# Retention of the second block: index scores, key choice and head finishing placed in pieces between the weight slabs

## Chip, cores and metric

The kernel runs on one core of one Trainium2 chip. The metric is the device time of one execution in microseconds (us).

## What is computed

Two transformer blocks for 512 tokens of width 1024 in fp32, one after the other. The second one works on 528 tokens (16 meta tokens in front): a SwiGLU, a mixer, a second SwiGLU and a norm. The change touches the mixer:

```python
proj = u @ w_in          # rq, rk, rv, rg, aq, ak, av, iq, ik, iw, g_ret, g_att
rq, rk = rope(rq), rope(rk) * RET_DK ** -0.5          # 4 heads of 256
yr = retention(rq, rk, rv)                            # decayed q k^T times v, 512 wide
yr = y * rsqrt(mean(y * y) + EPS)                     # at the end of retention, per head
yr = (silu(rg) * yr) @ w_ret_out
# index branch: which 128 keys a query may attend to
rel = relu(einsum('bqhd,bsd->bqhs', iq, ik))          # 8 heads of 64
score = einsum('bqh,bqhs->bqs', iw, rel) * idx_scale  # masked to earlier keys
_, sel = top_k(score, 128)
ya = attention(aq, ak, av, keys = meta + sel) @ w_att_out
merged = sigmoid(g_ret) * yr + sigmoid(g_att) * ya
out = merged @ w_mix_out
```

## The kernel before

**Slabs.** All projection weights come as slabs of 128 x 1024 fp32 (0.5 MB). SyncE's queue fetches them into six buffers (`raw_slabs`). ScalarE rounds each into one of four buffers (`slabs_rounded`, L1142, `split_ahead`), VectorE subtracts to get the remainder (`slabs_remainder`, L1744, `slab_remainder`), and TensorE multiplies: each product is the sum of three matmuls (rounded x rounded, rounded x remainder, remainder x rounded; L642, `Slab.add`). A slab of columns is 24 matmuls of 256 columns (272 in half 0), a slab of rows (values, `rows_of`) has matmuls of 512 columns: 12 in half 1, 18 in half 0. ScalarE may round slab q when TensorE has begun slab q - 3.

**The order.** Each engine runs its own program, written out by hand, in step with the others through semaphores. On ScalarE and VectorE a call of `point()` stands for one slab of TensorE's order: at slab t it prepares slab t + 3. What an engine has to do besides stands between the points, and holds back the points behind it.

**Two halves.** Block 2 runs twice: half 0 with 16 + 256 tokens (T = 272), half 1 with the other 256. During half 0 the first block's expert layer still goes on between the slabs (woven in by `woven_by`): GpSimd gathers a row of 2048 floats per token (L2484), VectorE takes a dot product (L1992) or, for every third row, also adds it up (L2041), ScalarE makes the coefficient and a diagonal matrix (L1295 to L1306), TensorE adds the row to its sums (L824, four matmuls of 512 columns). There, the projections have three PSUM banks (0 to 2); in half 1, where nothing is gathered, they have four (0 to 3), and the other products have banks 4 to 7.

**The mixer** (`mixer` of each engine). It begins with the index projections. Then come four retention heads of 12 slabs each: two query slabs, two key slabs, four value slabs, four gate slabs. Behind the query slabs VectorE ropes the queries (L2219 to L2229, `rope_pair`) and behind the key slabs the keys (in half 0, L2223 and L2224 read two banks); this frees the banks. After the key slabs of head 0 come the index scores: 16 matmul products with 64 rows (L957; 4 banks in half 0, 16 in half 1), relus of ScalarE out of PSUM (L1432), VectorE's weighted sum (L2181, L2187), the scale and the mask (L2195 to L2201). After the key slabs of head i > 0 TensorE sums the squares of head i - 1 (L967, `head_sums`) and VectorE finishes that head (`finish_head`): mean square (L2238), the root on ScalarE (L1419, `head_root`), reciprocal (L2243), two multiplies of 128 x 1024 (L2245, L2251). Then, in every head, VectorE makes four of the 16 rounds of key choice (`keep_keys`): MAX8 (L2208) finds the eight largest scores and MATCH_REPLACE8 (L2211) marks them. Only after that come the points of the four value slabs. After these TensorE computes the scores of the head (L996), VectorE multiplies in the decay (L2283, L2287), the gate slabs follow (L2300), then the value matmuls (L1008, L1011). After the four heads: four pairs of slabs for the retention gate (the last head is finished in the first pair, and the marks are turned into a mask, L2317 to L2320), 16 slabs of `w_ret_out` in four groups, merged with the gate (L2330), 8 value slabs, and the attention heads.

Of the kernel before, what the change touches and what calls it, by code (L numbers as in the profile page):

```python
# [16 lines left out]
P = 128  # L17
# [219 lines left out]
def index_heads(g):  # L237

    return (0, 2, 1, 3, 4, 6, 5, 7) if g == 2 else tuple(range(IDX_HEADS))

# [51 lines left out]
def build(nc, slabs_d, xT_d, memT_d, metaT_d, vecs_d, consts_d, consts16_d, subk_d, wi_d, peer_uv_d, out_d,  # L292
          n_slabs):
    ctx = ExitStack()
    with ctx:
# [313 lines left out]
        def _(pe):  # L609
# [276 lines left out]
            def two(x, off, n, since=None, per=1):  # L886

                b = claim(gm)
                for d in range(2):
                    one(x, off, n, b, d * n, None if d else since, per, d == 1)  # L890

            def rows_of(x, off, meta):
# [3 lines left out]
                for s in range(KT // 2):  # L896
                    w = slab()
# [31 lines left out]
            def mixer(h, r):  # L929
# [14 lines left out]
                def index_scores():  # L944
# [4 lines left out]
                    for j, tt in enumerate(h.judged):  # L949
                        w = (h.first + tt + 1) * P  # L950
                        g = 2 if 2 * w <= 512 else 1
                        for head in range(0, IDX_HEADS, g):
# [7 lines left out]
                            m.then_inc(bank_full[b], 1)  # L960

# [7 lines left out]

                for i in range(RET_HEADS):  # L970
                    two(x, h.off, HALF)
                    if h.off:
                        one(x, 0, h.T, claim(gm))
                        one(x, 0, h.T, claim(gm))
                    else:
                        two(x, 0, HALF)
                    if i == 0:
                        index_scores()
                    else:
                        head_sums(i - 1)  # L980
                    v_banks = rows_of(x, h.off, h.off)
# [133 lines left out]
        def _(act):  # L1115
# [297 lines left out]
            def mixer(h, r):  # L1413
# [7 lines left out]
                def index_relus():  # L1421
# [3 lines left out]
                    for j, tt in enumerate(h.judged):  # L1425
                        w = (h.first + tt + 1) * P
                        g = 2 if 2 * w <= 512 else 1
                        for head in range(0, IDX_HEADS, g):
# [5 lines left out]
                            n += 1  # L1434

# [7 lines left out]
                at.take()  # L1443
                for i in range(RET_HEADS):
                    n = RET_HEADS * h.n + i
                    gm.take()
                    for _ in range(2 if h.off else 1):
                        gm.take()
                    points(4)
                    if i == 0:  # L1450
                        index_relus()
                        act.wait_ge(index_scored, h.n + 1)
                        if h.n == 0:
                            keep(K_IK, r.ik, kept_index)
                    else:
                        head_root(i - 1)
                    banks = [gm.take(), gm.take()]
                    meta = at.take() if h.off else None
                    points(4)
# [188 lines left out]
        def _(dve):  # L1648
# [476 lines left out]
            def mixer(h, r):  # L2125
# [42 lines left out]
                def index_scores():  # L2168
# [24 lines left out]
                    dve.wait_ge(relu_read, n)  # L2193
# [39 lines left out]
                def finish_head(i):  # L2233
# [7 lines left out]
                    dve.sem_inc(ret_ms, 1)  # L2241
                    dve.wait_ge(ret_root, n + 1)
# [4 lines left out]
                                                  op0=ALU.mult, op1=ALU.mult))  # L2247
                    sync()
# [3 lines left out]

                for i in range(RET_HEADS):
# [7 lines left out]
                    points(2)  # L2261
# [3 lines left out]
                    if i == 0:  # L2265
                        index_scores()
                    else:
                        finish_head(i - 1)
                    for _ in range(KEEP // 8 // RET_HEADS):
                        keep_keys()  # L2270
# [3 lines left out]
                    points(4)  # L2274
# [19 lines left out]
                    for e in range(2):  # L2294
                        bn = gm.take()
                        points(2)
# [14 lines left out]
                for c in range(4):  # L2311
                    last_gate = gm.take()
                    points(2)
                    if c == 0:
                        finish_head(RET_HEADS - 1)
                        for j, w, tt in judged:
                            step(dve.tensor_scalar(work(tt, w), work(tt, w), TAKEN, HIDE, ALU.not_equal, ALU.mult))  # L2317
                        if h.n == 0:
                            step(dve.tensor_scalar(work(0, P), tri[:, :], -HIDE, HIDE, ALU.mult, ALU.add))
                        step(dve.memset(r.key_bias[:, :, 0:META], 0.0))  # L2320
                        sync()
                    elif c < 3:
                        rests(4 * c - 4, 4 * c)
                for c in range(4):
# [3 lines left out]
                    if c == 0:  # L2328
# [3 lines left out]
                                             op0=ALU.add, op1=ALU.mult).then_inc(bank_free[b], 1)  # L2332
                for _ in range(2):
# [311 lines left out]
```

## Time and profile before

| | us |
|---|---|
| median of 3 runs | 3811.61 (3810.2 to 3816.32) |
| profiled execution | 3811.19 |
| its span, first to last instruction | 3809.4 |
| TensorE busy | 3330.7 (87%) |
| VectorE busy | 2566.6 (67%) |
| ScalarE busy | 1521.3 (40%) |
| GpSimd busy | 872.7 (23%) |
| retention heads of half 0 | about 1898 to 2176 |
| retention heads of half 1 | about 3081 to 3337 |

The profile is of one execution. Its page gives busy times and the costliest groups of instructions. The trace behind it is asked for waits (which engine waited for what), for the chain of waits (from the last instruction back to what released each one), for timelines of one engine and for busy times by stretch. All times are counted from the start of the span. A wait for several semaphores is put down to the one that came last.

### The profile page before, as it was taken

What the parts mean: (1) busy time and instruction counts of PE and PEld (TensorE: products, weight loads), DVE (VectorE), ACT (ScalarE), POOL (GpSimd) and SP (SyncE); (2) the same over time, 40 slices, a digit from 0 to 9 for tenths busy, and PEclk for the clock granted to TensorE, in tenths of its full rate; (3) what the DMA queues carried; (4) which work ended last, traced back from release to release, by engine and by line L of the source; (5) the groups of instructions that cost most, each with busy time, mean ns of one, the idle gap of its engine ahead of it and who ended that gap; (6) DMA issues with size and microseconds to landing.
All of it is one profiled execution on the core that took longest, in us unless ns stands there. A gap on an engine that the chain in (4) does not pass through costs nothing.

```text
span 3809.4 us, 48792 instructions
## 1 busy us (share of the span) xinstructions
PE 3330.7 (87%) x17936; PEld 2570.4 (67%) x17936; DVE 2566.6 (67%) x4483; ACT 1521.3 (40%) x3015; POOL 872.7 (23%) x596
## 2 busy tenths in 40 slices
PE   6998979896777777699999999888979988899898
PEld 4886767682222222488777776667869977799898
DVE  5997241386676767687777677778765575558665
ACT  3222333323333333444444444544444433344443
POOL 1001333335656565222222232122100000000000
PEclk9999989998999999899999999999989999899999
DMA  3222222227999999699888898788746633253354
GB/s 110 94 94 72 83 83 85 72 83 324 420 382 418 385 421 397 261 381 388 344 315 322 306 388 341 284 320 343 301 148 224 193 115 115 97 177 120 124 187 155
DMA packets 178834, 901.87 MB, mean 237 GB/s; under 512 B 20944, under 2 KB 26320, under 8 KB 112672
## 3 DMA queue, kind: packets, MB, share of 16 engines
q0 software_dynamic: 73728, 536.90, 35.3%
q1 hardware_dynamic: 94640, 341.88, 26.0%
q10 hardware_dynamic: 10240, 20.12, 1.6%
q8 instruction: 136, 2.23, 0.2%
q14 instruction: 90, 0.74, 0.1%
HBM read 891.02 MB, written 7.80 MB: 236 GB/s over the span
## 4 chain that ended last, share of the span: by engine, by line
PE 63%; DVE 15%; DMA 7%; issue 7%; POOL 6%; ACT 3%; ACTq 0%; DVEq 0%; POOLq 0%
PE psum L642 49%; PE psum L824 8%; DMA buffer_float<-in_peer_uv,buffer_uint 6%; POOL buffer_float L2484 6%; DVE buffer_bfloat L1992 2%; PE psum L1011 1%; DVE buffer_float32r L1668 1%; DVE buffer_float L1705 1%; DVE slabs_remainder L1744 1%; DVE norm_mean_square L1698 1%; ACT slabs_rounded L1142 1%; PE psum L996 1%; DVE buffer_float L1941 1%; DVE norm_recip_root L1676 1%; PE psum L1093 1%
## 5 line engine op out<-in xcount | busy, mean ns | idle before, releaser
L642 PE MATMUL psum<-buffer_float32r,slabs_rounded 128*128 128x256 f32 (+2 forms) x9376 | 2026.4, 314 | 88.4 <-DVE buffer_float32r L1668 67.4
L642 PEld LDWEIGHTS psum<-buffer_float32r,slabs_rounded 128*128 128x128 f32 x9376 | 1534.3, 191 | 256.9 <-issue 149.6
L642 PE MATMUL psum<-buffer_float32r,slabs_remainder 128*128 128x256 f32 (+2 forms) x4688 | 1437.6, 307 | 0.0
L1744 DVE TENSOR_TENSOR slabs_remainder<-raw_slabs,slabs_rounded 128x1024 fp32r<-128x1024 f32 x570 | 695.7, 1224 | 498.5 <-ACT slabs_rounded L1142 491.9
L824 PE MATMUL psum<-buffer_float,buffer_float 128*128 128x512 f32 x1712 | 848.9, 624 | 186.1 <-ACT buffer_float L1306 159.3
L1142 ACT ACTIVATE slabs_rounded<-raw_slabs 128x1024 fp32r<-128x1024 f32 x650 | 683.5, 1056 | 738.0 <-PE psum L642 639.5
L2484 POOL DMA_INDIRECT buffer_float<-in_peer_uv,buffer_uint x512 | 679.2, 1327 | 1178.0 <-PE psum L824 650.3
L642 PEld LDWEIGHTS psum<-buffer_float32r,slabs_remainder 128*128 128x128 f32 x4688 | 895.4, 191 | 40.4
L1992 DVE CUSTOM_DVE_ANT_0 buffer_bfloat<-buffer_float,buffer_float 128x1024 bf16<-128x1024 f32 x512 | 625.8, 1222 | 236.9 <-DMA buffer_float<-in_peer_uv,buffer_uint 231.6
L824 PEld LDWEIGHTS psum<-buffer_float,buffer_float 128*128 128x128 f32 x1712 | 306.5, 196 | 614.7 <-issue 606.6
L2471 POOL TENSOR_TENSOR slabs_remainder<-raw_slabs,slabs_rounded 128x1024 fp32r<-128x1024 f32 x80 | 193.3, 2428 | 667.1 <-ACT slabs_rounded L1142 666.9
L1295 ACT ACTIVATE buffer_float<-buffer_float 128x1 f32<-128x1 f32 x512 | 100.9, 197 | 483.9 <-DVE buffer_float L1992 483.2
L642 PE MATMUL psum<-slabs_rounded,buffer_float32r 128*128 128x512 f32 (+1 forms) x608 | 192.7, 404 | 52.9 <-DVE slabs_remainder L1744 37.7
L1306 ACT ACTIVATE buffer_float<-fixed,buffer_float 128x128 f32<-128x128 f32 x428 | 172.0, 402 | 40.6 <-ACT buffer_float L1299 1.9
L642 PEld LDWEIGHTS psum<-slabs_rounded,buffer_float32r 128*128 128x128 f32 x608 | 116.4, 201 | 85.4 <-DVE slabs_remainder L1744 39.5
L1129 ACT ACTIVATE buffer_float32r<-buffer_float 128x256 fp32r<-128x256 f32 (+3 forms) x232 | 110.9, 495 | 137.7 <-DVE buffer_float L1705 55.7
L1782 DVE SCALAR_TENSOR_TENSOR buffer_float<-buffer_float,vecs,buffer_float 128x512 f32<-128x512 f32 x232 | 158.4, 748 | 0.0
L1299 ACT ACTIVATE buffer_float<-buffer_float,buffer_float 128x1 f32<-128x1 f32 x512 | 150.9, 295 | 16.9
L1668 DVE TENSOR_TENSOR buffer_float32r<-buffer_float,buffer_float32r 128x256 fp32r<-128x256 f32 (+2 forms) x232 | 118.7, 525 | 19.8 <-ACT buffer_float32r L1129 17.5
L642 PE MATMUL psum<-slabs_remainder,buffer_float32r 128*128 128x512 f32 (+1 forms) x304 | 117.6, 387 | 0.0
L2041 DVE SCALAR_TENSOR_TENSOR buffer_float<-buffer_float,buffer_float,buffer_float 128x1024 f32<-128x1024 f32 x82 | 105.1, 1282 | 0.0
L698 PE MATMUL psum<-norm_recip_root,fixed 128*128 128x256 f32 (+2 forms) x32 | 18.6, 673 | 96.2 <-DVE norm_recip_root L1676 86.4
(201 smaller groups left out, 1922.4 us busy)
## 6 DMA issues: line engine op xcount, KB each, us to landing
raw_slabs<-in_slabs SPq DMA_DIRECT2D x650, 512.0 KB, 3.7
buffer_float<-in_peer_uv,buffer_uint POOLq DMA_INDIRECT x512, 9.7
buffer_float<-kept ACTq DMA_DIRECT2D x1, 5248.0 KB, 17.9
xT<-in_xT ACTq DMA_DIRECT2D x4, 512.0 KB, 10.8
buffer_float<-in_consts ACTq DMA_DIRECT2D x8, 256.0 KB, 3.8
kept<-buffer_float ACTq DMA_DIRECT2D x4, 512.0 KB, 4.3
kept<-buffer_float ACTq DMA_DIRECT2D x4, 272.0 KB, 3.1
kept<-buffer_float ACTq DMA_DIRECT2D x8, 136.0 KB, 3.8
```

The costliest lines, as they stand in the source:

```text
L642: m = pe.matmul(out, a, b, start=start and j == 0, stop=stop and j == 2)
L824: m = pe.matmul(psum[:, b, :], diag[:, slot, :], uv_rows[slot][:, D + q * 512:D + (q + 1) * 512], start=p == 0, stop=p == PICKS - 1)
L1129: act.activation(dst, src, ACT.Copy).then_inc(rounded, 1)
L1142: act.activation(slab_h[:, j, :], raw[:, r, :], ACT.Copy).then_inc(slab_rounded, 1)
L1299: act.activation(coefs[:, slot:slot + 1], acts[:, slot:slot + 1], ACT.Copy, scale=gates[:, tt, p:p + 1])\
L1306: act.activation(diag[:, slot, :], ident[:, :], ACT.Copy, scale=coefs[:, slot:slot + 1])\
L1668: dve.tensor_tensor(dst, src, high.bitcast(F32), ALU.subtract).then_inc(split, 1)
L1744: dve.tensor_tensor(slab_l[:, r, :], raw[:, r, :], slab_h[:, j, :].bitcast(F32), ALU.subtract)\
L1782: step(dve.scalar_tensor_tensor(out=acc, in0=cfp[:, h, t:t + S], scalar=w, in1=acc, op0=ALU.mult, op1=ALU.add))
L1992: dve.tensor_tensor_reduce(dump, uv_rows[slot][:, 0:D], hrow[tt], 1.0, 0.0, ALU.mult, ALU.add, dots[:, slot:slot + 1]).then_inc(dotted, 1)
L2471: pool.tensor_tensor(slab_l[:, r, :], raw[:, r, :], slab_h[:, j, :].bitcast(F32), ALU.subtract)\
L2484: pool.indirect_dma_start(uv_rows[slot], None, peer_uv_d, bass.IndirectOffsetOnAxis(eidx[:, tt, p:p + 1], 0))\
```

## The change

It does these things, in both halves:

- TensorE (`index_scores` becomes a generator): the banks of index scores are computed some at a time, two before each of the two key slabs of head 0, and in half 1 also three before each of its four value slabs (`index_banks`). ScalarE's relus and VectorE's weighted sums stand in the same places, before the point of that slab. Scale and mask (`index_done`) come after the value slabs' points.
- ScalarE writes the index keys to memory after those points, and waits for their rope alone instead of for the finished scores.
- VectorE finishes head i - 1 in three pieces: the mean square after the key rope, as before; reciprocal and first multiply after the point of value slab 0; second multiply after that of value slab 1.
- The 16 rounds of key choice: none in head 0; in each of heads 1 to 3 one after the points of value slabs 2 and 3 and one between the two points of each gate pair; the last four after the four merged groups of `w_ret_out`.
- The marks are turned into the mask after these.

The diff (empty lines and some unchanged ones left out):

```diff
@@ -237,6 +237,11 @@
+def index_banks(h):
+    return (2, 3) if h.n else (2, 0)
@@ -883,17 +888,21 @@
-            def two(x, off, n, since=None, per=1):
+            def two(x, off, n, since=None, per=1, before=None):
...
                 for d in range(2):
+                    if before:
+                        before()
                     one(x, off, n, b, d * n, None if d else since, per, d == 1)
-            def rows_of(x, off, meta):
+            def rows_of(x, off, meta, before=None):
...
                 for s in range(KT // 2):
+                    if before:
+                        before()
                     w = slab()
@@ -958,6 +967,7 @@
                             m.then_inc(bank_full[b], 1)
+                            yield
@@ -967,18 +977,32 @@
+                scoring = index_scores()
+                def scores_in_k():
+                    for _ in range(index_banks(h)[0]):
+                        next(scoring)
+                def scores_in_v():
+                    for _ in range(index_banks(h)[1]):
+                        next(scoring)
...
                     if h.off:
-                        one(x, 0, h.T, claim(gm))
-                        one(x, 0, h.T, claim(gm))
+                        for _ in range(2):
+                            if i == 0:
+                                scores_in_k()
+                            one(x, 0, h.T, claim(gm))
                     else:
-                        two(x, 0, HALF)
+                        two(x, 0, HALF, before=None if i else scores_in_k)
+                    if i:
+                        head_sums(i - 1)
+                    v_banks = rows_of(x, h.off, h.off, None if i else scores_in_v)
                     if i == 0:
-                        index_scores()
-                    else:
-                        head_sums(i - 1)
-                    v_banks = rows_of(x, h.off, h.off)
+                        assert next(scoring, None) is None
                     own = [(r.rk, h.off + tt * P, r.rv[:, tt], tt * P) for tt in range(2)]
@@ -1432,6 +1456,7 @@
                             n += 1
+                            yield
@@ -1441,22 +1466,30 @@
                 at.take()
+                scoring = index_relus()
                 for i in range(RET_HEADS):
...
                     gm.take()
+                    points(2)
                     for _ in range(2 if h.off else 1):
                         gm.take()
-                    points(4)
-                    if i == 0:
-                        index_relus()
-                        act.wait_ge(index_scored, h.n + 1)
-                        if h.n == 0:
-                            keep(K_IK, r.ik, kept_index)
-                    else:
+                    for _ in range(2):
+                        for _ in range(0 if i else index_banks(h)[0]):
+                            next(scoring)
+                        point()
+                    if i:
                         head_root(i - 1)
...
                     meta = at.take() if h.off else None
-                    points(4)
+                    for _ in range(4):
+                        for _ in range(0 if i else index_banks(h)[1]):
+                            next(scoring)
+                        point()
+                    if i == 0:
+                        assert next(scoring, None) is None
+                        if h.n == 0:
+                            act.wait_ge(idx_rope, 3)
+                            keep(K_IK, r.ik, kept_index)
                     if h.off and i:
@@ -2190,7 +2223,12 @@
                             n += 1
-                    dve.wait_ge(relu_read, n)
+                            yield
+                def index_done():
+                    n = sum(IDX_HEADS // (2 if 2 * w <= 512 else 1) for _, w, _ in judged)
+                    dve.wait_ge(relu_read, 4 * h.n + n)
                     for j, w, tt in judged:
@@ -2239,17 +2277,20 @@
                     dve.sem_inc(ret_ms, 1)
+                    yield
                     dve.wait_ge(ret_root, n + 1)
...
                                                   op0=ALU.mult, op1=ALU.mult))
+                    yield
                     sync()
...
+                scoring = index_scores()
                 for i in range(RET_HEADS):
@@ -2258,20 +2299,30 @@
                     ks = [gm.take() for _ in range(2 if h.off else 1)]
-                    points(2)
+                    for _ in range(2):
+                        for _ in range(0 if i else index_banks(h)[0]):
+                            next(scoring)
+                        point()
                     if h.off and i:
...
                     rope_pair(r.rk, [full(bn) for bn in ks], h.T, 0)
-                    if i == 0:
-                        index_scores()
-                    else:
-                        finish_head(i - 1)
-                    for _ in range(KEEP // 8 // RET_HEADS):
-                        keep_keys()
+                    if i:
+                        finishing = finish_head(i - 1)
+                        next(finishing)
                     gm.take(), gm.take()
...
                         at.take()
-                    points(4)
+                    for p in range(4):
+                        for _ in range(0 if i else index_banks(h)[1]):
+                            next(scoring)
+                        point()
+                        if i and p < 2:
+                            next(finishing, None)
+                        elif i:
+                            keep_keys()
+                    if i == 0:
+                        assert next(scoring, None) is None
+                        index_done()
                     dve.wait_ge(decay_loaded, 32 * (n + 1))
@@ -2293,7 +2344,10 @@
                         bn = gm.take()
-                        points(2)
+                        point()
+                        if i:
+                            keep_keys()
+                        point()
                         b = full(bn)
@@ -2312,13 +2366,8 @@
                     if c == 0:
-                        finish_head(RET_HEADS - 1)
-                        for j, w, tt in judged:
-                            step(dve.tensor_scalar(work(tt, w), work(tt, w), TAKEN, HIDE, ALU.not_equal, ALU.mult))
-                        if h.n == 0:
-                            step(dve.tensor_scalar(work(0, P), tri[:, :], -HIDE, HIDE, ALU.mult, ALU.add))
-                        step(dve.memset(r.key_bias[:, :, 0:META], 0.0))
-                        sync()
+                        for _ in finish_head(RET_HEADS - 1):
+                            pass
                     elif c < 3:
@@ -2330,6 +2379,13 @@
                                              op0=ALU.add, op1=ALU.mult).then_inc(bank_free[b], 1)
+                    keep_keys()
+                for j, w, tt in judged:
+                    step(dve.tensor_scalar(work(tt, w), work(tt, w), TAKEN, HIDE, ALU.not_equal, ALU.mult))
+                if h.n == 0:
+                    step(dve.tensor_scalar(work(0, P), tri[:, :], -HIDE, HIDE, ALU.mult, ALU.add))
+                step(dve.memset(r.key_bias[:, :, 0:META], 0.0))
+                sync()
                 for _ in range(2):
```

## Rows read from the trace of the kernel before

**Rows 1.** The page: busy time by engine; two groups: busy us, mean ns | idle before.
```profile
PE 3330.7 (87%) x17936; PEld 2570.4 (67%) x17936; DVE 2566.6 (67%) x4483; ACT 1521.3 (40%) x3015; POOL 872.7 (23%) x596
...
L1744 DVE TENSOR_TENSOR slabs_remainder<-raw_slabs,slabs_rounded 128x1024 fp32r<-128x1024 f32 x570 | 695.7, 1224 | 498.5 <-ACT slabs_rounded L1142 491.9
...
L1142 ACT ACTIVATE slabs_rounded<-raw_slabs 128x1024 fp32r<-128x1024 f32 x650 | 683.5, 1056 | 738.0 <-PE psum L642 639.5
```

**Rows 2.** Waits of TensorE, 3070 to 3400 us: total, times, longest.
```profile
PE psum L642 <- DVE slabs_remainder L1744: 37.7, 4, 9.6
```

**Rows 3.** Chain of waits, 3150 to 3215 us: start us, us, what.
```profile
3153.02 11.37 PE psum L642 x96
3164.41 0.69 DVE buffer_float L2219
...
3167.72 1.76 DVE norm_mean_square L2243
...
3170.77 1.23 DVE buffer_float L2251
...
3182.82 1.24 DVE slabs_remainder L1744
...
3184.10 5.35 PE psum L642 x12
3189.45 4.20 PE psum L996 x20
3193.65 11.35 PE psum L642 x96
```

**Rows 4.** Busy time of three stretches: width, engines, granted clock, DMA share, GB/s.
```profile
3160.00:3190.00 30.00, 20.40 (x97) 16.41 (x96) 24.20 (x41) 8.01 (x9) 0.00 (x0) 0.83 0.31 104
3190.00:3220.00 30.00, 30.00 (x204) 26.92 (x203) 10.61 (x13) 10.87 (x14) 0.00 (x0) 1.00 0.35 114
...
1910.00:1925.00 15.00, 13.35 (x67) 10.02 (x66) 13.75 (x28) 4.65 (x10) 3.11 (x4) 0.89 0.93 373
```

**Rows 5.** Waits of TensorE, 1880 to 2260 us.
```profile
PE psum L824 <- ACT buffer_float L1306: 4.8, 2, 3.5
PE psum L824 <- issue: 4.5, 2, 2.9
PE psum L642 <- issue: 4.3, 2, 2.6
```

**Rows 6.** Timeline of TensorE in half 0: start, us, instruction [idle before].
```profile
1914.26 2.94 PE L957 MATMUL psum<-buffer_float,buffer_float 64*128 64x256 f32 x16
1918.85 3.21 PE L824 MATMUL psum<-buffer_float,buffer_float 128*128 128x512 f32 x4 [1.65 <-issue]
...
1990.42 0.71 PE L642 MATMUL psum<-slabs_rounded,buffer_float32r 128*128 128x512 f32 x2 [2.57 <-issue]
```

**Rows 7.** Timeline of VectorE in half 0.
```profile
1918.25 0.43 DVE L2224 TENSOR_TENSOR buffer_float<-psum,buffer_float 128x272 f32<-128x272 f32 x1
...
1919.87 0.35 DVE L2181 TENSOR_SCALAR buffer_float<-buffer_float,buffer_float 128x256 f32<-128x256 f32 x1
1920.25 3.83 DVE L2187 SCALAR_TENSOR_TENSOR buffer_float<-buffer_float,buffer_float,buffer_float 128x256 f32<-128x256 f32 x7
...
1925.35 0.43 DVE L2208 MAX8 buffer_float<-buffer_float 128x8 f32<-128x256 f32 x1
...
1926.55 0.43 DVE L2208 MAX8 buffer_float<-buffer_float 128x8 f32<-128x256 f32 x1
...
1989.84 0.43 DVE L2224 TENSOR_TENSOR buffer_float<-psum,buffer_float 128x272 f32<-128x272 f32 x1
```

**Rows 8.** L957 alone, in its two stretches of half 1: width, PE and PEld busy.
```profile
3093.07:3095.86 2.79, 2.78 (x12) 1.28 (x12) 1.00 0.04 15
3097.53:3105.31 7.78, 7.77 (x20) 2.95 (x20) 1.00 0.00 0
```

**Rows 9.** Waits of VectorE, 1880 to 2260 us.
```profile
DVE buffer_bfloat L1992 <- DMA buffer_float<-in_peer_uv,buffer_uint: 20.5, 13, 3.8
```

## The prediction

> **What bounds the kernel now.** I read the page first [rows 1]: TensorE is busy for 87% of a span of 3809.4 us and is the engine on which the chain mostly runs, so an edit pays only where TensorE stands still or runs at the lower clock. The edit touches the retention of block 2, which runs once per half of the tokens. So I took TensorE's waits in the two stretches, the chain of waits in the second, and then single instructions of VectorE.
>
> Half 1 (3060 to 3410 us): TensorE waits 37.7 us in four waits of up to 9.6 us, and all four are for a slab remainder of VectorE [rows 2]. One of them in the chain [rows 3]: VectorE ropes the keys from 3164.41, finishes the head before (mean square, reciprocal at 3167.72, two wide multiplies), does four rounds of key choice from 3172.00 on, 2.7 us each, and only then, at 3182.82, makes the remainder that the fourth value slab waits for; TensorE resumes at 3184.10. VectorE is not short of time: in 3190 to 3220 us it is busy 10.6 us of 30 [rows 4]. It does 18 us of other work in one piece, while only three slabs of 2.8 us are prepared ahead. The wait costs more than itself: in the stretch with the wait the mean granted clock is 0.83 against 1.00 in the next [rows 4], so part of it is at the lower of the two levels (1.2 instead of 2.4 GHz), and the fourth value slab takes 5.35 us [rows 3].
>
> Half 0 (1880 to 2260 us) is another case: expert rows are gathered and added between the slabs there. TensorE waits 13.6 us in six waits, none for a remainder [rows 5]. At head 0 it stops at 1917.20, after the index matmuls (1914.26 + 2.94), and goes on at 1918.85; at head 1 it goes on at 1990.42 after 2.57 us [rows 6]. In both cases VectorE's four reads of the key banks have just ended: at 1918.68 and at 1990.27 [rows 7]. Half 0 has only three banks for projections, and the second value bank is a key bank: the value slabs can't start before the keys are roped. The finishing and the key choice come behind that rope, and while VectorE does them (1919 to 1930 us) TensorE has its prepared slabs and these of 4.2 us or more (18 matmuls in half 0, and gathered rows between). They cost nothing there today.
>
> **Half 1, heads 1 to 3.** The change removes no instruction; it puts a slab remainder between the pieces. I walk one head from the start of its first query slab, with four slabs in 11.35 us, so 2.8 us a slab, and score matmuls of 4.20 us [rows 3]. Head sums and three value slabs fill 10.1 us (from 11.37 us after 3153.02 to 9.6 us before 3184.10), so the head sums take 1.7 us. TensorE without waits: value slabs at 13.1, 15.9, 18.7 and 21.3, scores at 24.1, gate slabs at 28.3, 31.1, 34.0 and 36.8. VectorE: key rope and mean square as now, and the root is back at 14.7 (3167.72). Behind the root ScalarE rounds the fourth value slab (1.06 us, [rows 1]) and VectorE's remainder (1.22 us, [rows 1]) is ready at 17.0; needed at 21.3. Reciprocal and first multiply (3.05 us) to 20.1, next remainder (gate slab 0) 21.3, second multiply (1.23 us) 22.5, remainder 23.7, one choice 26.4, remainder 27.6, one choice 30.3, five decay multiplies of at most 256 columns (0.43 us each, the row of L2224 [rows 7]) 32.5, the remainder of the last gate slab 33.7; needed at 36.8. That is the tightest place, 3.1 us to spare; the others have 4 to 7. The two choices between gate slabs end at about 43, and the next head begins at 49, after the value matmuls, so they are covered. ScalarE's gate tanh waits for the finished head (22.5) and needs its bank only at 34: covered. So both parts of the cost go: 9.6 us of wait and 5.35 - 2.8 = 2.55 us of slow slab, 12.15 us a head, **36.4 us** for three.
>
> **Half 1, head 0.** Now 12 index matmuls take 2.78 us, and after a wait of 1.7 us 20 more take 7.77 us [rows 8]: 12.2 us. Then come three value slabs, a wait of 8.9 us (37.7 less three of 9.6) and the slow slab (2.5 us). After the change two banks stand before each key slab and three before each value slab. Cost on TensorE alone: not under 2.78 / 6 = 0.46 us a bank, 7.4 us for 16; not over today's 12.2 us. The 20 paced by VectorE give 0.78 us a bank for the wider ones; I take 8 x 0.46 + 8 x 0.72 = 9.5 us, nearer to the lower end because slabs now cover ScalarE's copies. VectorE has three banks of 0.78 us and a remainder of 1.22 us in each value step, 3.6 us, against 3 x 0.6 + 2.8 = 4.6 us on TensorE. Gain 8.9 + 2.5 + 2.7 = **14.1 us** (11.4 to 16.2). The choice rounds of head 0 move behind the last gate: four, each after one merged pair. There TensorE has four slabs of 2.8 us per pair and VectorE 4 x 1.22 us, a multiply of this size out of PSUM (0.69 us, as at 3164.41 [rows 3]) and 2.7 us, 8.3 in all: hidden, with three slabs ready when the choice starts. If that cover failed, each could cost up to 2.7 us, 11 us.
>
> The TensorEngine Tiling page of the Trainium skill (Key Properties) says that a change of tiling mode drains TensorE; the change enters and leaves the 64-row form six times per half 1 instead of once, and twice in half 0. The trace of before shows one entry and one exit a half, both inside the 12.2 us and the 2.94 us above. By the page twelve more drains would make the time longer, by what a drain costs, which no row isolates; the upper bound of 12.2 us holds it, and the sum stays.
>
> **Half 0, head 0.** Here the change adds. The index matmuls (2.94 us, [rows 6]) move ahead of the key slabs, and VectorE's scoring (from 1919.87 to 1924.08, 4.2 us [rows 7]) moves ahead of the key rope, on which the value slabs wait. VectorE is busy nearly without a break there: 13.75 of 15 us from 1910 to 1925 [rows 4]. So the banks are read out some 4.1 us later (1922.8 instead of 1918.7), and the matmuls that used to fill that time are done before: TensorE idles about 5.8 us in place of 1.65. Behind it VectorE is 6 us ahead of today, which buys nothing, since nothing was late. Bounds: 0, if VectorE catches up before the key slabs end, and 4.2 + 2.94 = 7.1 us, if scoring and index matmuls add in series; a gain has no place, since nothing that ends the wait comes earlier. Taken, near the row that VectorE is full: +4.1 us, and +0.4 us for a longer stay at the lower clock (the 1.65 us wait already made four matmuls take 3.21 us [rows 6]).
>
> **Half 0, the rest.** Heads 1 to 3 keep the same wait for the rope; the pieces behind it are only interleaved: 0. The four choices that go behind the gates are 1.2 us each (1925.35 to 1926.55 [rows 7]), between a gathered row and its dot, in a stretch where VectorE waits for gathers (20.5 us in 13 waits [rows 9]). Between 0 and 4.8 us; I take +0.5. The mask multiplies move from the first gate to behind the last: 0, with 0.5 us of VectorE at stake.
>
> **Sum.** -36.4 - 14.1 + 4.5 + 0.5 = -45.5 us. The profiled execution took 3811.2 us (3809.4 us of span); the median of the runs shown is 3811.6, 0.4 us above. 3811.6 - 45.5 = 3766 us, 1.2% faster.
>
> **The rivals.**
> A. Part of the stall comes back. For: 3.1 us to spare before the last gate slab, and ScalarE's rounding now stands behind relus and the root. If a wait of 2.5 us with 2.5 us of slow clock stays in each of four heads, 20 us are lost: 3786 us.
> B. The gathers of half 0 lose more. For: dots wait for landings in 13 places. If each of the ten choices moved next to gate slabs or merges (six and four) holds up a row by its 1.2 us, 12 us in place of 0.5: 3777 us.
> C. Half 0 gains as well: its waits (13.6 us) close and head 0 costs nothing, because the gathers bound it and absorb the delay: 3811.6 - 50.5 - 13.6 = 3748 us. Against: the waits end with the rope.
> D. The wait of half 1 isn't VectorE's order but moves with it: at the end of its pieces VectorE is again more than three slabs (8.5 us) late, before the last gate slab, in each head. Then 9.6 + 2.5 us stay per head, and half 0 pays 5 us and B's 11.5: 3828 us, slower. It decides from 3.1 us more VectorE work before that slab for any wait at all, and from some 13 us for the whole of it; the walk leaves no place for 13 us.
> E. The change doesn't do what it says (the wait is put down wrongly to the remainder and stays): 3811.6 + 5 = 3817 us, within 0.2%. Against: all four have the same pattern.
>
> **How the numbers follow.** Forecast 0.62, A 0.13, B 0.10, C 0.08, D 0.03, E 0.04. Range: downwards the forecast with its bounds (head 0 at -16.2, half 0 at 0) is 3759, and some way to C; upwards through B to A: 3755 to 3788. Two tenths are left for C's end, the outer part of A, D and E. What a measurement of this kernel can tell from no change is about 0.2% or 7.6 us: faster 0.93, same 0.04, slower 0.03.
>
> **What would show it.** Right: in half 1 TensorE's waits for remainders fall from 37.7 us to under 3, heads follow each other in 49.2 us instead of 61.3, the value slabs run at 1.00 granted clock, choice rounds stand singly between remainders. In half 0 the wait before the value slabs of head 0 grows from 1.65 to about 5.8 us, the others stay at 1.7 to 2.9. Wrong: a wait for a remainder before the last gate slab (A, D), longer waits for landings after 2220 us (B), or no longer wait at head 0 of half 0 (C).

## The result

| | before | after |
|---|---|---|
| median, us | 3813.28 (3810.2 to 3816.32, 4 runs) | 3767.48 (3763.24 to 3771.78, 4 runs) |
| ratio | | 0.9879, 95% interval 0.9866 to 0.9892 |
| span of the profiled execution | 3809.4 | 3761.4 |

The change makes the kernel 1.2% faster, 45.8 us by the medians and 48.0 us by the two spans. The forecast was 3766 us, 45.5 us less. By the interval the gain lies between 41 and 51 us.

In half 1 the stall is gone. Where [rows 2] had 37.7 us of waits for a remainder, the waits of TensorE in the profile of the change from 3070 to 3360 us are an empty list. The chain of waits of the change from 3144 to 3195 us (start us, us, what) now stays on TensorE through the whole of head 1, where [rows 3] went over VectorE for 20 us:

```profile
3144.16 11.36 PE psum L647 x96
3155.52 1.73 PE psum L977 x8
3157.24 11.20 PE psum L647 x48
3168.44 4.20 PE psum L1020 x20
3172.64 11.36 PE psum L647 x96
...
3193.35 1.65 PE psum L647 x14
```

(L647 are the slabs, L977 the head sums, L1020 the scores; L642, L967 and L996 of before.) Four value slabs take 11.20 us without a break. From head to head it is 49.19 us (3144.16 to 3193.35) instead of the 61.3 us of before. The busy time by stretch of the change, in the head of the chain above and behind it (width, PE, PEld, DVE, ACT, POOL, granted clock, DMA share, GB/s) shows VectorE busy in both stretches, for 25.7 and 20.1 us, and the clock at 1.00 in both. In [rows 4] the stretch with the wait has 0.83 and the next one 1.00:

```profile
3160.00:3190.00 30.00, 30.00 (x179) 25.34 (x178) 25.74 (x42) 12.08 (x14) 0.00 (x0) 1.00 0.38 124
3190.00:3220.00 30.00, 30.00 (x179) 25.81 (x178) 20.10 (x26) 12.25 (x14) 0.00 (x0) 1.00 0.45 150
```

The timeline of VectorE in the change, in that head (start, us, instruction), shows how: a remainder (L1777) stands between the pieces, which are reciprocal (L2282) with the first multiply (L2284), the second multiply (L2291), and each choice (L2246, L2249).

```profile
3160.96 1.75 DVE L2282 RECIPROCAL norm_mean_square<-norm_recip_root 128x256 f32<-128x256 f32 x1
3162.74 1.23 DVE L2284 SCALAR_TENSOR_TENSOR buffer_float<-buffer_float,norm_mean_square 128x1024 f32<-128x1024 f32 x1
3163.88 1.22 DVE L1777 TENSOR_TENSOR slabs_remainder<-raw_slabs,slabs_rounded 128x1024 fp32r<-128x1024 f32 x1
3165.02 1.22 DVE L2291 TENSOR_TENSOR buffer_float<-buffer_float,buffer_float 128x1024 f32<-128x1024 f32 x1
3166.15 1.22 DVE L1777 TENSOR_TENSOR slabs_remainder<-raw_slabs,slabs_rounded 128x1024 fp32r<-128x1024 f32 x1
3167.29 1.15 DVE L2246 MAX8 buffer_float<-buffer_float 128x8 f32<-128x384 f32 x2
...
3175.73 1.21 DVE L1777 TENSOR_TENSOR slabs_remainder<-raw_slabs,slabs_rounded 128x1024 fp32r<-128x1024 f32 x1
```

In half 0 the wait before the value slabs of head 0 has grown. First the chain of waits of the change, on TensorE; before, [rows 6] had a wait of 1.65 us there:

```profile
1911.83 1.07 PE psum L966 x8
1912.90 3.20 PE psum L647 x24
1916.10 6.41 issue
1922.52 3.75 PE psum L829 x4
```

VectorE's timeline in the change, in the same stretch; before, [rows 7] had the rope's last read at 1918.25:

```profile
1911.19 0.35 DVE L2214 TENSOR_SCALAR buffer_float<-buffer_float,buffer_float 128x256 f32<-128x256 f32 x1
...
1916.57 2.11 DVE L2220 SCALAR_TENSOR_TENSOR buffer_float<-buffer_float,buffer_float,buffer_float 128x256 f32<-128x256 f32 x4
...
1921.92 0.43 DVE L2262 TENSOR_TENSOR buffer_float<-psum,buffer_float 128x272 f32<-128x272 f32 x1
```

The scoring (L2214, L2220) stands ahead of the key rope, whose last read of a bank (L2262) is 3.7 us later than before and ends at 1922.35. TensorE idles 6.41 us and goes on at 1922.52. Its next four matmuls take 3.75 us; the granted clock from 1922.5 to 1926.3 is 0.50, the lower level.

To see where time goes and comes back, one can compare when the same matmul of the slabs starts in each trace. Each column is the difference to before, in us; the runs of the last columns are described below.

```
place (start in before)              change  half1_only  half0_only  scores_late_half0  rope_first
half 0, head 0, 1st value slab done  +4.8    +0.5        +5.5        -0.5               -3.9      (1932.4)
half 0, first gate pairs             +3.6    +4.0        +7.5        -1.2               -10.2     (2202.4)
end of half 0's mixer and after      +0.4    -0.2        +2.9        -3.2               -11.7     (2593.0)
half 1, head 0, key slabs            +4.4    +2.5        +5.3        -0.9               -10.8     (3083.0)
half 1, retention gate               -45.4   -47.6       +6.2        -51.1              -61.2     (3320.5)
last matmul                          -48.0   -50.3       +6.4        -53.8              -64.0     (3795.7)
```

(The label's last number is the place's start in the trace of before.) The stretch between the first and the third row is not the same twice even for one piece of code (all differences are to the one profile of before): half1_only has the order of before in half 0, and is 4.0 us behind at one place and 0.2 us ahead at the next. Six profiles with the change's code in half 0 have +0.4, +2.8, +2.9, +6.0, +6.8 and +6.8 us in the third row. From its key slabs on, half 1 repeats: the eight profiles with the change's order there gain 49.7 to 50.5 us between the fourth row and the fifth. Heads 1 to 3 alone (3132.1 to 3320.5 of before) gain 36.57 us in each of these eight and in scores_late_half1.

### The profile page after: what moved, and what is told of

It is laid out like the page before. It is cut to its first block, busy times and chain, and to the rows that moved or that the text cites. A ratio compares the mean times of both kernels' runs of the same rounds, so it can differ in the third digit from the quotient of the medians.

```text
span 3761.4 us, 48792 instructions
## 1 busy us (share of the span) xinstructions
PE 3318.8 (88%) x17936; PEld 2560.1 (68%) x17936; DVE 2562.1 (68%) x4483; ACT 1519.6 (40%) x3015; POOL 866.5 (23%) x596
## 4 chain that ended last, share of the span: by engine, by line
PE 66%; DVE 12%; DMA 7%; issue 6%; POOL 6%; ACT 3%; ACTq 0%; DVEq 0%; POOLq 0%
PE psum L647 51%; PE psum L829 8%; DMA buffer_float<-in_peer_uv,buffer_uint 6%; POOL buffer_float L2540 6%; DVE buffer_bfloat L2025 2%; DMA raw_slabs<-in_slabs 1%; PE psum L1035 1%; DVE norm_mean_square L1731 1%; ACT slabs_rounded L1166 1%; DVE buffer_float L1738 1%; DVE buffer_float32r L1701 1%; PE psum L1020 1%; DVE buffer_float L1974 1%; DVE norm_recip_root L1709 1%; PE psum L1117 1%
## 5 line engine op out<-in xcount | busy, mean ns | idle before, releaser
L647 PE MATMUL psum<-buffer_float32r,slabs_rounded 128*128 128x256 f32 (+2 forms) x9376 | 2027.6, 314 | 89.5 <-DVE buffer_float32r L1701 67.6
L647 PEld LDWEIGHTS psum<-buffer_float32r,slabs_rounded 128*128 128x128 f32 x9376 | 1533.4, 191 | 260.6 <-issue 152.2
L647 PE MATMUL psum<-buffer_float32r,slabs_remainder 128*128 128x256 f32 (+2 forms) x4688 | 1436.1, 306 | 0.0
L1777 DVE TENSOR_TENSOR slabs_remainder<-raw_slabs,slabs_rounded 128x1024 fp32r<-128x1024 f32 x570 | 696.5, 1224 | 505.9 <-ACT slabs_rounded L1166 497.5
L647 PEld LDWEIGHTS psum<-buffer_float32r,slabs_remainder 128*128 128x128 f32 x4688 | 895.0, 191 | 40.7
L647 PE MATMUL psum<-slabs_rounded,buffer_float32r 128*128 128x512 f32 (+1 forms) x608 | 184.8, 390 | 14.3 <-POOL slabs_remainder L2527 10.9
L647 PEld LDWEIGHTS psum<-slabs_rounded,buffer_float32r 128*128 128x128 f32 x608 | 111.6, 193 | 46.0 <-issue 15.2
L1701 DVE TENSOR_TENSOR buffer_float32r<-buffer_float,buffer_float32r 128x256 fp32r<-128x256 f32 (+2 forms) x232 | 118.7, 526 | 20.1 <-ACT buffer_float32r L1153 17.8
L647 PE MATMUL psum<-slabs_remainder,buffer_float32r 128*128 128x512 f32 (+1 forms) x304 | 113.9, 375 | 0.0
## 6 DMA issues: line engine op xcount, KB each, us to landing
xT<-in_xT ACTq DMA_DIRECT2D x4, 512.0 KB, 10.6
```

Source lines behind the costliest of these rows:

```text
L647: m = pe.matmul(out, a, b, start=start and j == 0, stop=stop and j == 2)
L1701: dve.tensor_tensor(dst, src, high.bitcast(F32), ALU.subtract).then_inc(split, 1)
L1777: dve.tensor_tensor(slab_l[:, r, :], raw[:, r, :], slab_h[:, j, :].bitcast(F32), ALU.subtract)\
```

## The experiments

Each run was measured beside executions of the kernel before. Their medians are 3812.3, 3812.8 and 3813.0 us in the three groups of runs, and 3813.3 us beside the change. The change itself was not measured again, so a comparison with it is across groups. One kernel measured twice in this way (rope_first, rope_first_again) gave 3753.8 and 3749.2 us. So a difference under about 5 us between two runs needs the traces beside it.

**One half at a time.** The variants share one file in which the number of score banks before the key slabs, behind them and before the value slabs is a triple, and finishing and choices can be whole or in pieces, for each half.

half1_only:
```diff
-    return (2, 3) if h.n else (2, 0)
+    return (2, 0, 3) if h.n else (0, 4, 0)     # key slabs, behind them, value slabs
+PIECES = (False, True)
```

> The change in half 1 alone, half 0 in the order of before. Theory 1 (a ledger by stretch: half 1 gives 49 us, half 0 costs 4 to 5 us up to 2200 us, and the stretch behind it, bound by gathers, gives all but 0.5 us back): 48 to 49 us less than before, about 1 us less than the full change. Theory 2 (the pieces of half 0 earn what its early scores cost): the same as the full change, 46 to 48 us less than before. Rival to both (half 0's delay is paid for in full): 5 us less than the full change, 51 us less than before.

Measured: 3763.07 us, ratio 0.987 (0.9853 to 0.9886), 49.2 us less than before. That is nearest to theory 1, but the interval (44 to 56 us less) leaves the rival in and theory 2 too.

half0_only:
```diff
+    return (0, 16, 0) if h.n else (2, 0, 0)
+PIECES = (True, False)
```

> The change in half 0 alone, half 1 in the order of before. Theory 1: TensorE 4 to 5 us later than before at 2200 us, 0 to 1 us later from 2320 us on; the whole within 1 us of before. Theory 2: later by 4 us only up to the second head, nothing left at 2200 us. If the delay is paid for in full: 5 us longer than before at the end. In half 1 all four waits for remainders are there, 37.7 us.

Measured: 3816.56 us, ratio 1.0009 (0.9999 to 1.0018), 4.3 us more than before, in 10 runs against 14; the interval just takes in no change. Half 0's cost is there in the trace (first row, +5.5), and TensorE ends 6.4 us late. The waits of TensorE in half0_only from 3060 to 3420 us (engine, line, waited for: us, times, longest us) have the four of before again:

```profile
PE psum L650 <- DVE slabs_remainder L1785: 37.7, 4, 9.6
```

So the gain is half 1's. Theory 1 had it from the one profile of the change that half 0's cost is given back behind it: that profile has the smallest third row of the six. In the mean of the six the cost at the end of half 0 is 4.3 us, and it is 4.3 us by these medians. This speaks against theory 1, though neither settles it: the six spread over 6.4 us and stand against one profile of before. The next run gives more.

**Scores late in half 0.**
```diff
+    return (2, 0, 3) if h.n else (0, 4, 0)
```

> The full change, but in half 0 all four banks of index scores stay behind the key slabs and VectorE's scoring behind the key rope. Theory 1: the wait before the value slabs of head 0 is 1.7 us again instead of 6.4, TensorE is 4 us ahead of the full change until 2200 us, and behind the gather-bound stretch less than 1 us ahead: 47 us less than before. Theory 2: the 4 us stay: 51 us less than before.

Measured: 3757.79 us, ratio 0.9855 (0.9839 to 0.9872), 54.5 us less than before (49 to 61), and its last matmul is 5.9 us ahead of the change's. The wait before the value slabs of head 0, 6.41 us in the change, is back to that of before, by the waits of TensorE in this run from 1900 to 1935 us:

```profile
PE psum L829 <- issue: 1.7, 1, 1.7
```

Theory 1's 47 us lie outside the interval and theory 2's 51 us inside it: the cost of the early scores isn't given back. With half0_only and rope_first_early (below) three comparisons by medians say so, by 4.3 to 8.7 us, each run taken against its own before; each of them alone is weak. That the pieces of half 0 earn something of their own is a hint only: with scores late they put this run 3 us ahead of half1_only in the third row and 3.5 us in the last, which is within the spread of that stretch.

**Pieces off in half 1.** PIECES = (True, False), score banks as in the change.

> The full change, but in half 1 heads 1 to 3 finish the head before and make four choices in one piece behind the key rope, as before (scores stay between the slabs, the four choices of head 0 stay behind the gates). If the wait was this one piece: 9.6 us of wait and 2.5 us of slow slab come back in each of three heads, 36.4 us more than the full change, 11 us less than before. If the scores had been part of it in these heads too, less than 36 us comes back.

Measured: 3799.87 us, ratio 0.9965 (0.995 to 0.9979), 12.4 us less than before. Three waits are back, by the waits of TensorE in this run from 3060 to 3420 us:

```profile
PE psum L650 <- DVE slabs_remainder L1780: 29.1, 3, 9.9
```

The chain of waits of the same run shows one, with 5.49 us for the slab behind it:

```profile
3180.46 1.24 DVE slabs_remainder L1780
...
3181.74 5.49 PE psum L650 x12
```

Its profile is of the slowest of its five executions (3810.8 us) and is 10.6 us behind before at the key slabs already, so the stretch is counted from behind these. From 3105.2 to 3320.5 of before it gains 4.2 us where the change gains 41.9: 37.7 us for three heads, against 36.4 in my sum. The one piece of VectorE work was the wait.

**Scores late in half 1.** `return (0, 16, 0) if h.n else (2, 0, 0)`, pieces on in both halves.

> The full change, but in half 1 all 16 banks of index scores stay between the key slabs and the value slabs of head 0, as before; finishing and choices in pieces, no choice in head 0. My theory: TensorE spends 12.2 us on them again where it spends 9.1 us now in the full change, and VectorE's scoring ends before the fourth value slab is due (no choice behind it), so the wait of 8.9 us shrinks to under 1 us: 3 to 5 us more than the full change. Rival: the placing of the scores had removed the wait of head 0, and most of 8.9 + 2.5 us comes back: 12 to 14 us more.

Measured: 3769.81 us, ratio 0.9889 (0.9866 to 0.9911). No wait for a remainder is back, only the one for a relu between the index matmuls (waits of TensorE in this run, 3060 to 3420 us):

```profile
PE psum L966 <- ACT buffer_float L1459: 1.7, 1, 1.7
```

From 3083.0 to 3132.1 of before it gains 11.4 us, the change 13.3. So putting the scores between the slabs is worth 1.9 us in the traces, where 3 to 5 us were expected (2.8 us by the medians); the rest of head 0's gain comes with the choices leaving it. The rival's 12 to 14 us are out.

**How much slack.** Idle MAX8 instructions on VectorE, ahead of the decay multiplies in heads 1 to 3 of half 1:

```diff
+                    if h.n and i:
+                        for _ in range(4):        # 11 in slack_9us
+                            step(dve.max(r.top8[:, 1, :], work(1, 4 * P)))
+                            sync()
```

> The full change, with four idle MAX8 of 128x512 on VectorE (0.8 us each with their wait, 3.2 us) before the decay multiplies of heads 1 to 3 in half 1; their result is not used. In the trace of the full change the remainder of the last gate slab is ready at 3176.94 and the slab begins at 3180.9, 4.0 us of slack (my walk had 3.1). If the walk's reading is right, 3.2 us more cost nothing: no wait for a remainder in half 1, head after head 49.2 us. If VectorE's total load were the limit, each head would be 3 us longer.

Measured: 3770.53 us (one run), no wait for a remainder in half 1, and its heads start at 3123.98, 3173.16 and 3222.35: 49.18 us each, as in the change. The 2.9 us (4 x 0.73) disappear in the slack.

> The same with eleven idle MAX8, 8.9 us. Only what is over 4.0 us shows: a wait for the remainder of the last gate slab of 4.9 us in each of heads 1 to 3, and up to 2.5 us of low clock behind it, 15 to 22 us in all. If the slack were a matter of the head's total, no wait would come, since VectorE is idle for over 8 us later in the same head.

Measured: 3778.84 us (one run), and three waits, in the list of TensorE's waits from 3060 to 3420 us:

```profile
PE psum L647 <- DVE slabs_remainder L1777: 11.7, 3, 4.1
```

The chain of waits of this run shows the first of them, in front of the last gate slab:

```profile
3179.80 0.70 DVE buffer_float L2328
...
3182.39 1.14 DVE slabs_remainder L1777
...
3183.57 5.49 PE psum L647 x24
```

Each idle MAX8 turned out to take 0.73 us, so 8.0 us were put in. In the change the remainder for this slab is ready at 3176.94 (3175.73 + 1.21, above) and the slab starts at 3172.64 + 3 x 2.84 = 3181.16: 4.2 us to spare. That leaves 3.8 us, and the waits are 3.8 to 4.1 us. The slabs behind them take 5.49, 4.44 and 4.63 us instead of 2.84. From 3105.2 to 3337.2 of before this run loses 18.2 us to the change, within the 15 to 22 forecast. What counts is how late VectorE is at one place, not how busy it is over the head.

**The rope first.** The waits before the value slabs of half 0 looked like waits for the key rope. VectorE's point of the second key slab (a remainder, a dot, sometimes a row) is put behind the rope, in half 0:

```diff
-                        point()
+                        if h.n or _k == 0:
+                            point()
...
                     rope_pair(r.rk, [full(bn) for bn in ks], h.T, 0)
+                    if h.n == 0:
+                        point()
```

> Scores late in half 0 as in the run before, and there VectorE ropes the keys before the point of the second key slab, not behind it, in all four heads. Theory: the waits of 1.7 to 2.9 us before the value slabs of half 0 are for that rope, which stands behind a remainder, a dot and a row of 3.7 us; they shrink to under 0.5 us, TensorE is 7 to 9 us ahead of the run before at 2200 us, and the end is 4 to 9 us earlier (3749 to 3754 us beside a before of 3812). Rival: the gathers bound half 0, the waits move to the rows, and the end is the same within 1 us.

Measured: 3753.83 us, ratio 0.9853 (0.9834 to 0.9873), 4.0 us less than scores_late_half0, and 9.0 us ahead of it in the second row of the table, as the theory had it. The waits before the value slabs are gone; of half 0's waits one is left, at the first gate pair (waits of TensorE in this run, 1880 to 2260 us):

```profile
PE psum L829 <- ACT buffer_float L1333: 4.3, 1, 4.3
```

> The kernel of the run rope_first once more, beside the others on one chip: 59 us less than before (57 to 64).

The second time: 3749.23 us, ratio 0.9839 (0.9824 to 0.9854), 63.8 us less than before. This version, with the scores late in half 0, the rope first and everything else as in the change, is faster than before by 1.6%, and than the change by 0.4% going by the two ratios. In the third row of the table it stands at -11.9 us, where rope_first has -11.7.

> Half 1 as in the full change. Half 0: scores late, finishing and choices whole as before, and the keys roped before the point of the second key slab. It differs from the next run only in the pieces of half 0. If the pieces are worth 3 us there (what one profile and the medians hint at), 3 us longer than the next; if they are worth nothing, as I forecast, the same within 1.5 us at the end of half 0.

Measured: 3751.21 us, ratio 0.9838 (0.9825 to 0.9852). In the third row it stands at -6.7 us, 5 us behind its neighbour, but the medians differ by 2.0 us and the ratios by nothing. In the second row it is 1.3 us ahead, and the stretch in between is the one that doesn't repeat. What the pieces of half 0 are worth stays open, between 0 and 5 us.

> The full change with the keys roped before the point of the second key slab in half 0, and the scores early, as in the change. VectorE's scoring still stands before the key rope of head 0, so about 4 us of wait stay before the value slabs of head 0 and none in heads 1 to 3: 4 to 5 us longer than rope_first_again. If the rope alone had been at fault, no difference.

Measured: 3753.82 us, ratio 0.9853 (0.9837 to 0.9868), 4.6 us more than rope_first_again. Its waits in half 0 (1880 to 2260 us) are the two below; the first stands before the value slabs of head 0. The early scores cost with the rope first as well: 3.6 us of wait, and 4.4 and 7.4 us in the first row against the two profiles of rope_first. The 4.6 us by medians are no more than what rope_first differs from itself, so here the traces carry it.

```profile
PE psum L829 <- issue: 3.6, 1, 3.6
PE psum L829 <- ACT buffer_float L1330: 3.4, 1, 3.4
```

> The kernel before, changed in this alone: in half 0 the keys are roped before the point of the second key slab. The three or four waits before value slabs go (9 us with their slow clock): 8 to 11 us less than before at 2200 us and at the end. If the gathers bound half 0, nothing is left at the end.

Measured: 3806.39 us, ratio 0.9984 (0.9974 to 0.9993), 6.6 us less than before; -5.2, -8.4 and -6.2 us in the second, third and last row. Less than the 8 to 11 us expected, but clear of no change, so the gathers don't take it all back.

## Why the prediction was right

- **Heads 1 to 3 of half 1: -36.4 us.** From score to score it is three times 49.19 us instead of 184.1 us in all: -36.6 us. Both parts were as read, the wait and the half-speed slab behind it. The walk put the tightest place before the last gate slab with 3.1 us to spare; it is there, with 4.2 us. (Of the 1.1 us between them 0.2 are a slip of the walk: 11.4 + 10.1 puts the fourth value slab at 21.5, not 21.3, and all behind it too.)
- **Head 0 of half 1: -14.1 us.** From the end of the index weights to the scores it took 46.4 us and takes 34.0: -12.4 us. The index matmuls cost 8.7 us of TensorE in six groups, 0.54 us a bank, where I had 9.5, so the sum should have come to 14.9, 2.5 too much. Two things that it didn't hold come to 2.7 us. The clock is at 0.72 from 3084 to 3090 us, in the two query slabs ahead, 1.6 us that the trace of before doesn't have; TensorE has no wait just before it. And the six groups cost some 1.1 us around themselves (last section). The term stayed inside its bounds of 11.4 to 16.2.
- **Half 0, head 0: +4.5 us.** Right in kind and 1 us short at its place: counted from 1890 us on, where the change was 0.8 us ahead already, it cost 5.6 us in the profile of the change and 5.5 in half0_only (4.0 to 5.6 in the six profiles). The step that carries it, that scoring would stand in front of the rope and TensorE behind it, is what the timeline shows; 6.41 us of wait for 5.8. I had written that this part costs; scores_late_half0 shows that the change would have been better without it.
- **Half 0, the rest: +0.5 us.** Not to be told apart. Waits of VectorE for gathered rows from 1880 to 2260 us went from 20.5 us [rows 9] to 9.0, and are 9.0 to 14.9 in the six profiles, so rival B has nothing for it. The pieces may even gain there.
- **What the sum didn't hold.** From the retention gate to the end the change gains 2.5 us more, in attention heads that it doesn't touch (next section but one). The profile of the change is 1.4 us ahead in its first 300 us too, in code that is the same.
- **How near the number came.** The mechanism and the large terms were right. That the medians meet the forecast to 0.3 us is luck beside: the interval is 10 us wide, half 0's term came out between 0.4 and 6.8 us from profile to profile, and 2.5 us of the gain come from a stretch that the sum didn't hold.
- **The rivals.** A, D and E are out: no wait for a remainder is left, and slack_9us shows what A would look like. C is out: the waits of half 0 stayed, and the early scores cost. Its idea, that those waits are for the rope, led to rope_first.

## What to carry to other kernels

When an engine prepares work a fixed number of steps ahead, its other work must be cut so that no piece between two preparations is longer than that lead; its share of busy time says nothing on this. A wait costs the slow clock behind it too: 2.5 us behind waits of 9.6 us, and still 1.6 to 2.7 us behind the waits of 4 us in slack_9us. And before work is moved ahead of something, look at which instruction behind it frees a bank: here early scores gain 1.9 us in half 1 and cost 4 to 6 us in half 0, where the value slabs wait for the rope. That the third bank against the fourth makes this difference is argued from the code; it wasn't tried alone.

## What the hardware showed beside

**The same wait, another clock.** In the attention heads of half 1 TensorE waits 2.68 us at the same instruction in both traces. TensorE's timeline, first of before, then of the change (start, us, instruction, and in brackets the wait ahead of it):

```profile
3533.39 3.00 PE L1057 MATMUL psum<-buffer_float,buffer_float 128*128 128x272 f32 x10 [2.68 <-DVEq L2350]
```

```profile
3487.89 2.35 PE L1081 MATMUL psum<-buffer_float,buffer_float 128*128 128x272 f32 x6 [2.68 <-DVEq L2406]
```

The busy time of the 40 us around each, first of before, then of the change:

```profile
3525.00:3565.00 40.00, 34.40 (x226) 31.39 (x226) 22.23 (x37) 15.53 (x29) 0.00 (x0) 0.87 0.31 97
```

```profile
3477.00:3517.00 40.00, 34.40 (x248) 31.82 (x248) 24.72 (x44) 17.50 (x32) 0.00 (x0) 0.96 0.31 103
```

Ten matmuls in 3.00 us stand against six in 2.35 us, but PE is busy for 34.40 us of both stretches, and the granted clock is 0.87 in the one and 0.96 in the other: 3.2 us are gained there. The same 3.2 us are gained in seven of the profiles, and nothing in slack_3us and scores_late_half1. slack_3us has the change's code from there on and comes to the place 4.6 us later. So whether the clock falls behind a wait of this length seems to hang on when the wait comes; what decides was not tried.

**What a group of 64-row matmuls costs around itself.** In half 1 of the change the group between the first two value slabs starts 0.32 us after the last matmul of the slab before it, where slab matmuls follow each other in 0.23, and the slab's first matmul has 0.10 us more behind it than the others. A value slab between two groups takes 2.99 us (3101.69 to 3104.68) instead of 2.80. So six groups cost about 1.1 us beside their own time. The TensorEngine Tiling page of the Trainium skill (Key Properties) says that a change of tiling mode drains TensorE; these 0.19 us on a slab are what this case's trace shows beside a group. Whether they are that drain the trace doesn't tell.
